# Three pairs of down units per late expert and MLP group as seven half-size products

## The chip, the cores and the metric

The kernel runs on one core of a Trainium2 chip. The metric is the device time of one execution in microseconds (us). The engines are TensorE (PE, with its weight loads PEld), VectorE (DVE), ScalarE (ACT), GpSimd (POOL) and SyncE (SP), which issues the transfers. The median of the kernel before is 3008.59 us over 3 runs, 3008.18 to 3008.73.

## What is computed

The reference is two transformer-like blocks over 512 tokens of 1024 features, in float32. The first has attention, retention and a feed-forward over 16384 experts (`peer_ffn`); the second has an RWKV-7 branch, a convolution, attention over a memory and an ordinary MLP. The two parts that matter here both have the form "multiply up, activate, scale, multiply down, add to x":

```python
# experts (each token gates 8 heads x 16 of the 16384 experts; all others have gate 0)
act = jax.nn.gelu(jnp.einsum('thkd,td->thk', u, xb), approximate=False)
out = jnp.einsum('thk,thkd->td', gate * act, v)
# MLP of the second block
x = x + jnp.square(jax.nn.relu(hm @ w_up)) @ w_down
```

## The kernel before

All of x lies in SBUF as 8 chunks of 128 features by 512 tokens (`x`, C = 8, P = 128, T = 512). The experts are computed densely: all 16384 in 16 groups of 1024, with the gates of the tokens in a table that is zero where an expert isn't chosen. The MLP has 4 groups of 1024 hidden features.

A weight unit is 128 x 1024 floats: 8 chunks of 128x128. `Weights` (L52 on) holds a ring of RING = 4 raw units. A unit is split into two parts of a shorter float format, because a product is then three fast matmuls: ScalarE copies it into the high part (`hi_step`, L142), VectorE subtracts to get the low part (`lo_step`, L150), and TensorE multiplies high x high, high x low and low x high for each of the 8 chunks (`multiply`, L184; `multiply_chunk`, L170), 24 matmuls of 512 tokens. The input side has high and low parts too (`act_hi`, `act_lo`, `inner_hi`, `inner_lo`). High and low parts are made AHEAD = 2 units before their use. SyncE loads the next unit into a raw slot once the low part of the unit that was in it is made (`load`, L111).

`feed_forward` (L1591 on) runs the last 8 of the 16 expert groups and all 4 MLP groups. Each group has 16 units: first 8 up units into PSUM banks 0 to 3, then 8 down units into banks 4 to 7, one per output chunk of x. For each up unit VectorE scales the product by `rstd` (L1705), ScalarE applies the activation (L1675), VectorE multiplies by the gate (experts) or by itself (MLP) (L1717), ScalarE copies the high part (L1677), and VectorE subtracts the low part (L1719), into chunk k of `inner`. For each down unit VectorE adds the PSUM bank to its chunk of x (L1726). The two activation tiles `raw_act` and `raw_gated` each have two buffers. All orders are written out by hand: an engine has one loop over the groups, each wait names a count of a semaphore, and the value is computed in the loop. The last group of each call is written out separately, with the first steps of what follows it (`following`, the RWKV input) or ends it (`final`). On SyncE each expert group also loads the gates of the next group, 2 MB (L1616), after the load of its 16th unit. GpSimd has nothing in these groups.

What stands ahead: in the early expert groups (`stored_groups`) GpSimd multiplies stored up products by `rstd` (L1819). In the RWKV part, GpSimd multiplies convolution inputs (L2354). In the gate stage GpSimd multiplies one-hot tiles (L1473), while VectorE makes others from a PSUM tile (L1556, L1563). In the memory attention units are multiplied with 256 tokens (L184 with `branch_hi`).

## Time and profile before

| | |
|---|---|
| median of 3 runs | 3008.59 us |
| span of the profiled execution | 3009.3 us |
| TensorE busy | 2968.3 us (99%), 15858 matmuls |
| VectorE busy | 1718.1 us (57%) |
| ScalarE busy | 1063.5 us (35%) |
| GpSimd busy | 440.2 us (15%) |
| high part of a unit, ScalarE L142 | 459 times, 1053 ns each |
| low part of a unit, VectorE L150 | 399 times, 1258 ns each |
| down products of late groups, L170 with inner | 3 x 1024 matmuls, 395 ns each |

The span is from the first to the last instruction of one execution taken by the profiler; it lies 0.7 us above the median of the runs. A matmul's record is longer than its share of time, as matmuls are pipelined: their distance from start to start counts. The 8 late expert groups begin at about 1231 us of the span and take 89.6 us each; the MLP groups lie between 2641 and 2996 us.

### The profile page before, as it was taken

To read this page: it belongs to the slowest core of one execution; us is meant where nothing else is said; L and a number is where in the kernel's file an instruction comes from. 1 tells how busy PE (TensorE), PEld (TensorE's weight loads), DVE (VectorE), ACT (ScalarE), POOL (GpSimd) and SP (SyncE) were. 2 spreads that over 40 slices of the span, in tenths; PEclk is the share of its full clock that TensorE was granted. 3 is DMA by queue.
4 is the path that set the end of the run, shared out by engine and by line. 5 is a ranking of instruction groups with operands and counts; after the bars stand their busy time and mean duration, and the time that the engine had idled before them with its cause. 6 is when DMAs were issued, how large, how long until landed. Compare 5 with 4: busy or idle time off the path is not lost. (4 is left out here: it accounts for less than half of the span.)

```text
span 3009.3 us, 42541 instructions
## 1 busy us (share of the span) xinstructions
PE 2968.3 (99%) x15858; PEld 2378.4 (79%) x15858; DVE 1718.1 (57%) x3031; ACT 1063.5 (35%) x1537; POOL 440.2 (15%) x317
## 2 busy tenths in 40 slices
PE   9999999999999999999999999999999999999998
PEld 7656888889978888788888888786896888778886
DVE  4665389999836556444444444666455464544444
ACT  3355123244443433222233322424225252433222
POOL 0200055565542231000000000020220000000000
PEclk9999999999999999999999999999999999999999
DMA  4212234455575464333333233322002233222221
GB/s 141 91 52 72 83 113 129 144 183 223 223 266 189 159 216 174 96 126 118 125 125 120 83 125 125 93 89 65 28 3 84 91 119 112 71 90 92 86 95 70
DMA packets 107065, 353.03 MB, mean 117 GB/s; under 512 B 11682, under 2 KB 12706, under 8 KB 105411
## 3 DMA queue, kind: packets, MB, share of 16 engines
q1 hardware_dynamic: 106946, 351.42, 34.8%
q8 instruction: 79, 1.29, 0.2%
q14 instruction: 40, 0.32, 0.0%
HBM read 298.95 MB, written 52.43 MB: 117 GB/s over the span
## 5 line engine op out<-in xcount | busy, mean ns | idle before, releaser
L142 ACT ACTIVATE weights_hi<-weights_raw 128x1024 fp32r<-128x1024 f32 x459 | 479.9, 1053 | 759.1 <-PE psum L170 386.9
L184 PE MATMUL psum<-act_hi,weights_hi 128*128 128x512 f32 x1592 | 632.0, 397 | 4.2 <-PEq L1317 1.7
L184 PE MATMUL psum<-act_lo,weights_hi 128*128 128x512 f32 x1592 | 628.9, 395 | 0.0
L184 PE MATMUL psum<-act_hi,weights_lo 128*128 128x512 f32 x1592 | 628.8, 395 | 0.0
L150 DVE TENSOR_TENSOR weights_lo<-weights_raw,weights_hi 128x1024 fp32r<-128x1024 f32 x399 | 500.2, 1258 | 105.7 <-ACT weights_hi L142 105.3
L170 PE MATMUL psum<-inner_hi,weights_lo 128*128 128x512 f32 x1024 | 404.5, 395 | 0.0
L170 PE MATMUL psum<-inner_hi,weights_hi 128*128 128x512 f32 x1024 | 404.5, 395 | 0.0
L170 PE MATMUL psum<-inner_lo,weights_hi 128*128 128x512 f32 x1024 | 404.5, 395 | 0.0
L184 PEld LDWEIGHTS psum<-act_hi,weights_hi 128*128 128x128 f32 x1592 | 298.4, 187 | 80.5 <-issue 7.7
L184 PEld LDWEIGHTS psum<-act_lo,weights_hi 128*128 128x128 f32 x1592 | 298.5, 187 | 73.2 <-issue 1.2
L184 PEld LDWEIGHTS psum<-act_hi,weights_lo 128*128 128x128 f32 x1592 | 298.4, 187 | 73.0
L1726 DVE TENSOR_TENSOR x<-x,psum 128x512 f32<-128x512 f32 x96 | 66.1, 688 | 304.8 <-PE psum L170 304.8
L170 PEld LDWEIGHTS psum<-inner_hi,weights_lo 128*128 128x128 f32 x1024 | 191.9, 187 | 47.1
L170 PEld LDWEIGHTS psum<-inner_lo,weights_hi 128*128 128x128 f32 x1024 | 191.9, 187 | 47.0
L170 PEld LDWEIGHTS psum<-inner_hi,weights_hi 128*128 128x128 f32 x1024 | 191.9, 187 | 46.9
L150 POOL TENSOR_TENSOR weights_lo<-weights_raw,weights_hi 128x1024 fp32r<-128x1024 f32 x44 | 116.2, 2648 | 271.4 <-ACT weights_hi L142 271.4
L1402 PEld LDWEIGHTS psum<-hot 128*128 128x128 f32 x1024 | 133.8, 191 | 12.2
L2055 POOL TENSOR_TENSOR gates_of_group<-rwkv_projections 128x512 f32<-128x512 f32 x15 | 22.2, 1483 | 783.2 <-DVE rwkv_projections L2017 783.2
L1402 PE MATMUL psum<-hot 128*128 128x128 f32 x1024 | 134.7, 274 | 0.0
L1819 POOL TENSOR_TENSOR up_group<-up_group,rstd 128x512 f32<-128x512 f32 x64 | 95.2, 1524 | 221.7 <-DMA up_group<-ups_dram 219.9
L1556 DVE TENSOR_TENSOR hot<-psum,picks_t 128x512 f32<-128x512 f32 x192 | 125.4, 688 | 3.4 <-PEq L1391 2.2
L1876 DVE TENSOR_TENSOR x<-x,psum 128x512 f32<-128x512 f32 x64 | 44.1, 689 | 144.3 <-PE psum L170 144.3
(425 smaller groups left out, 4378.0 us busy)
## 6 DMA issues: line engine op xcount, KB each, us to landing
weights_raw<-in_u_experts SPq DMA_DIRECT2D x256, 512.0 KB, 3.6
gates_dram<-gates_stage SPq DMA_DIRECT2D x8, 4096.0 KB, 12.2
gates_of_group<-gates_dram SPq DMA_DIRECT2D x16, 2048.0 KB, 11.8
weights_raw<-in_u_mlp SPq DMA_DIRECT2D x64, 512.0 KB, 3.4
ups_dram<-up_products SPq DMA_DIRECT2D x64, 256.0 KB, 2.2
up_group<-ups_dram SPq DMA_DIRECT2D x8, 2048.0 KB, 8.9
weights_raw<-in_u_in SPq DMA_DIRECT2D x24, 512.0 KB, 4.2
weights_raw<-in_u_merge SPq DMA_DIRECT2D x24, 512.0 KB, 3.6
```

The lines of the kernel that those rows point to most:

```text
L142: self.nc.scalar.activation(self.hi[slot][:, :, :], self.raw[:, slot, :].rearrange("p (c n) -> p c n", c=C), ACT.Copy).then_inc(self.hi_re ...
L150: eng.tensor_tensor(self.lo[slot][:, :, :], self.raw[:, slot, :].rearrange("p (c n) -> p c n", c=C), self.hi[slot][:, :, :].bitcast(F32), ...
L170: mm = self.nc.tensor.matmul(out, w[slot][:, c, :], a[:, c, :], start=c == 0 and n == 0, stop=c == C - 1 and n == 2)
L184: mm = self.nc.tensor.matmul(out, w[slot][:, c, :], a[:, j, 0:tokens], start=first and n == 1, stop=last and n == 3 * len(chunks))
L1402: mm = nc.tensor.matmul(psum[:, k, t * P:(t + 1) * P], hot1[c % HOTS][:, t, :], hot2[c % HOTS][:, t, :], start=True, stop=True)
L1556: return nc.vector.tensor_tensor(hot[:, :, :], places_of_keys.unsqueeze(1).to_broadcast([P, QUAD, P]), picks_t[:, r, bass.ds(i * LOOP_TOKE ...
L1726: nc.vector.tensor_tensor(x[:, d, :], x[:, d, :], psum[:, 4 + d % RING, :], ALU.add).then_inc(out_free.sem, 1)
L1819: nc.gpsimd.tensor_tensor(group[:, c, :], group[:, c, :], rstd[:], ALU.mult).then_inc(ups_scaled.sem, 1)
L1876: nc.vector.tensor_tensor(x[:, d, :], x[:, d, :], psum[:, 4 + d % RING, :], ALU.add).then_inc(out_free.sem, 1)
L2055: nc.gpsimd.tensor_tensor(self.diff[:, n % 2, :], rw[:, n, 0:T], rw[:, n, 1:T + 1], ALU.subtract).then_inc(shift_diff.sem, 1)
```

## The change

In `feed_forward` every group but the last of each call keeps its 8 up units and its first PLAIN = 2 down units. The other six down units form PAIRS = 3 pairs, A (units 10, 11), B (12, 13) and C (14, 15). A pair is a matrix of 2 x 2 weight blocks (two output chunks by the even and the odd halves of the inner chunks) times a matrix of 2 x 2 blocks of the inner activations (even and odd chunks by two halves of 256 tokens). Instead of eight block products it takes seven, by Winograd's form of Strassen's scheme. Each product is 4 x 3 = 12 matmuls of 256 columns. The names are P1 to P7; A11, A12 are the blocks of the upper unit, A21, A22 of the lower; S1 = A21 + A22, S2 = S1 - A11, S3 = A11 - A21, S4 = A12 - S2 are the weight sums, T1 to T4 the token sums.

What each engine does in such a group:

- GpSimd: 4 weight sums per pair, 128x512 each, from the raw units (`weight_sums`).
- VectorE: per pair of inner chunks one subtraction of 512 elements and two of 256 (`token_sums`) in the activation buffers, then one low part of 1024 elements (`tokens_lo`); per pair of units one low part of 1024 and five of 512; per pair five adds of 256 and one of 512 to x.
- ScalarE: one high part of 1024 elements per pair of inner chunks (`tokens_hi`); per pair of units one of 1024 and five of 512.
- TensorE: 8 up units, 2 plain down units, 3 x 84 matmuls of 256 columns, in a written order that interleaves the pairs.

The high and low parts of S1 and A22 lie in the ring's slot of the lower unit; S2, S3 and S4 have tiles of their own, which are laid where the RWKV and the convolution tiles lie later or lay before. The gate is applied in place, and `raw_act` and `raw_gated` together are now four buffers. In the first call the small RWKV loads wait until the last group has begun, and so do GpSimd's first steps of what follows.

```diff
-                        for d in range(C):
-                            pe.wait_ge(out_free.sem, i * C + (base + d + 1))
-                            bank = psum[:, 4 + d % RING, :]
-                            for c in range(C):
-                                if d == 0:
-                                    pe.wait_ge(ffn_lo.sem, i * C + (h0 + c + 1))
-                                mm = w.multiply_chunk(pe, i, C + d, per, bank, (h_hi, h_lo), c)
-                            mm.then_inc(w.unit_done.sem, 1)
+                    def product(out, weight, part, start=False, stop=False):
+                        for q in range(Q):
+                            for n, (a, b) in enumerate(((0, 0), (0, 1), (1, 0))):
+                                mm = nc.tensor.matmul(out, weight(q)[a], part(q)[b], start=start and q == 0 and n == 0,
+                                                       stop=stop and q == Q - 1 and n == 2, skip_group_check=True)
+                        return mm
...
+                    def p5(i, p):
+                        after(pe, fast_lo, LOWS, i, p, "S1")
+                        if p == A_:
+                            pe.wait_ge(t_lo_ready.sem, i * Q + (t_lo_ready.base + Q))
+                        product(beside(p, 1), unit_part(slots_of(p)[1], 0), token_sum(T1), start=True).then_inc(fast_product.sem, 1)
...
+                    def p6(i, p):
+                        after(pe, fast_lo, LOWS, i, p, "S2")
+                        after(pe, fast_read, READS, i, p, 1)
+                        product(chain(p), weight_sum(2), token_sum(T2)).then_inc(fast_product.sem, 1)
...
+                    def group(i, lead=None):
+                        ups(i, lead)
+                        for d in range(PLAIN):
+                            plain(i, d, RING - 2)
+                        p1(i, A_)
+                        p5(i, A_)
+                        p6(i, A_)
+                        p2(i, A_)
+                        p3(i, A_)
+                        p1(i, B_)
+                        p7(i, A_)
+                        p5(i, B_)
+                        p6(i, B_)
+                        p4(i, A_)
+                        p2(i, B_)
+                        p3(i, B_)
+                        p1(i, C_)
+                        p7(i, B_)
+                        p5(i, C_)
+                        p6(i, C_)
+                        p4(i, B_)
+                        p2(i, C_)
+                        p7(i, C_)
+                        p3(i, C_)
+                        p4(i, C_)
...
+                    def token_sums(i, q):
+                        pair = raw_pair(q)
+                        upper, lower = (pair[:, n, :].rearrange("p (h t) -> p h t", h=2) for n in range(2))
+                        dve.wait_ge(ffn_lo.sem, i * C + (h0 + 2 * q + 2))
+                        nc.vector.tensor_tensor(upper, pair[:, :, H:T], upper, ALU.subtract).then_inc(t_first.sem, 1)
+                        dve.wait_ge(t_first.sem, i * Q + (t_first.base + q + 1))
+                        nc.vector.tensor_tensor(lower[:, 1, :], lower[:, 1, :], upper[:, 0, :], ALU.subtract).then_inc(t_second.sem, 1)
+                        dve.wait_ge(t_second.sem, i * Q + (t_second.base + q + 1))
+                        nc.vector.tensor_tensor(lower[:, 0, :], lower[:, 0, :], lower[:, 1, :], ALU.subtract).then_inc(t_summed.sem, 1)
...
+                    def fast_body(i):
+                        for k in range(C):
+                            scale(i, k)
+                            if k and k % 2 == 0:
+                                token_sums(i, k // 2 - 1)
+                            elif 1 < k < C - 1:
+                                tokens_lo(i, k // 2 - 1)
+                            gate(i, k)
+                            if k < C - 1:
+                                w.lo_step(dve, i, k + w.AHEAD, per)
+                            inner_lo_step(i, k)
+                        w.lo_step(dve, i, C - 1 + w.AHEAD, per)
+                        tokens_lo(i, Q - 2)
+                        a1_lo(i, A_)
+                        token_sums(i, Q - 1)
+                        add_plain(i, 0)
+                        s1_lo(i, A_)
+                        a22_lo(i, A_)
+                        tokens_lo(i, Q - 1)
+                        s2_lo(i, A_)
+                        add_plain(i, 1)
+                        add_p1(i, A_)
+                        s4_lo(i, A_)
+                        add_p5(i, A_)
+                        s3_lo(i, A_)
+                        a1_lo(i, B_)
+                        s1_lo(i, B_)
+                        a22_lo(i, B_)
+                        add_u2(i, A_)
+                        s2_lo(i, B_)
+                        add_upper(i, A_)
+                        s4_lo(i, B_)
+                        add_p1(i, B_)
...
+                    def weight_sums(i, p):
+                        (k0, k1), (slot0, slot1) = units_of(p), slots_of(p)
...
+                        loaded(pool, i, k0)
+                        loaded(pool, i, k1)
+                        if p:
+                            after(pool, fast_lo, LOWS, i, p - 1, "S1")
+                        nc.gpsimd.tensor_tensor(s1, a21, a22, ALU.add).then_inc(s_summed.sem, 1)
+                        if p:
+                            after(pool, fast_lo, LOWS, i, p - 1, "S2")
+                        after(pool, s_summed, SUMS, i, p, 1)
+                        nc.gpsimd.tensor_tensor(s2, s1, a11, ALU.subtract).then_inc(s_summed.sem, 1)
+                        if p:
+                            unit_ready(pool, w.lo_ready, i, units_of(p - 1)[1])
+                        nc.gpsimd.tensor_tensor(s3, a11, a21, ALU.subtract).then_inc(s_summed.sem, 1)
+                        after(pool, s_summed, SUMS, i, p, 2)
+                        nc.gpsimd.tensor_tensor(s4, a12, s2, ALU.subtract).then_inc(s_summed.sem, 1)
```

## Rows read from the trace of the kernel before

**Rows 1.** Page, busy time: us, share of the span, instructions.
```profile
PE 2968.3 (99%) x15858; PEld 2378.4 (79%) x15858; DVE 1718.1 (57%) x3031; ACT 1063.5 (35%) x1537; POOL 440.2 (15%) x317
```

**Rows 2.** Busy time by stretch: stretch, length, each engine's busy us, clock, DMA share, GB/s.
```profile
1455.20:1500.00 44.80, 44.80 (x194) 35.99 (x193) 17.02 (x19) 10.61 (x11) 0.00 (x0) 1.00 0.45 152
1410.40:1455.20 44.80, 44.80 (x194) 35.99 (x193) 22.54 (x29) 15.51 (x21) 0.00 (x0) 1.00 0.27 82
```

**Rows 3.** Chain in order of time, two halves of MLP groups: start, us, what.
```profile
2725.93 44.80 PE psum L184 x192
2770.73 44.80 PE psum L170 x192
```

**Rows 4.** Timeline, first and last of 96 matmuls: start, us, engine, line, operation.
```profile
2464.56 0.28 PE L184 MATMUL psum<-branch_hi,weights_hi 128*128 128x256 f32 x1
...
2475.64 0.28 PE L184 MATMUL psum<-branch_hi,weights_lo 128*128 128x256 f32 x1
```

**Rows 5.** Timeline of VectorE, then ScalarE, after an eighth up unit (over at 1455.20).
```profile
1455.39 0.69 DVE L1705 TENSOR_TENSOR inner_activated<-psum,rstd 128x512 f32<-128x512 f32 x1 [1.78 <-PE psum L184]
1456.78 0.69 DVE L1717 TENSOR_TENSOR inner_gated<-inner_activated,gates_of_group 128x512 f32<-128x512 f32 x1 [0.70 <-ACT inner_activated L1675]
1458.17 0.69 DVE L1719 TENSOR_TENSOR inner_lo<-inner_gated,inner_hi 128x512 fp32r<-128x512 f32 x1 [0.70 <-ACT inner_hi L1677]
1458.78 2.36 DVE L150 TENSOR_TENSOR weights_lo<-weights_raw,weights_hi 128x1024 fp32r<-128x1024 f32 x2
...
1456.11 0.63 ACT L1675 ACTIVATE inner_activated<-inner_activated 128x512 f32<-128x512 f32 x1 [2.28 <-DVE inner_activated L1705]
1457.50 0.63 ACT L1677 ACTIVATE inner_hi<-inner_gated 128x512 fp32r<-128x512 f32 x1 [0.76 <-DVE inner_gated L1717]
1458.04 1.99 ACT L142 ACTIVATE weights_hi<-weights_raw 128x1024 fp32r<-128x1024 f32 x2
```

**Rows 6.** Timeline, a VectorE operation of 256 elements.
```profile
2479.65 0.42 DVE L3311 TENSOR_TENSOR conv_out<-psum,memory_rstd 128x256 f32<-128x256 f32 x1 [1.31 <-PE psum L184]
```

**Rows 7.** One line's instructions, GpSimd L1819: ns minimum/median/maximum.
```profile
L1819 POOL TENSOR_TENSOR up_group<-up_group,rstd x64: 1279/1296/2307, 848.4 to 1162.1; 128x512 f32<-128x512 f32 x64
```

**Rows 8.** Timeline of VectorE, then GpSimd, in an early expert group.
```profile
972.61 2.13 DVE L150 TENSOR_TENSOR weights_lo<-weights_raw,weights_hi 128x1024 fp32r<-128x1024 f32 x1
...
972.36 1.29 POOL L1819 TENSOR_TENSOR up_group<-up_group,rstd 128x512 f32<-128x512 f32 x1 [33.00 <-DMA up_group<-ups_dram]
...
973.61 2.27 POOL L1819 TENSOR_TENSOR up_group<-up_group,rstd 128x512 f32<-128x512 f32 x1
```

**Rows 9.** Timeline of VectorE and GpSimd in the RWKV part (first and last of four).
```profile
2089.43 0.69 DVE L2285 TENSOR_TENSOR rwkv_b<-rwkv_b,decay_inverse 128x512 f32<-128x512 f32 x1
2089.60 3.47 POOL L2354 TENSOR_TENSOR conv_projections<-conv_projections 128x512 f32<-128x512 f32 x1 [24.76 <-DVE conv_projections L2297]
...
2091.24 0.69 DVE L2288 SCALAR_TENSOR_TENSOR rwkv_kk<-rwkv_kk,decay_before 128x512 f32<-128x512 f32 x1
2092.01 2.14 DVE L150 TENSOR_TENSOR weights_lo<-weights_raw,weights_hi 128x1024 fp32r<-128x1024 f32 x1
```

**Rows 10.** GpSimd L1473 (ns minimum/median/maximum), and busy time in its stretch.
```profile
L1473 POOL TENSOR_TENSOR hot<-hot,picks_t x64: 1038/1040/1047, 619.9 to 819.2; 128x512 f32<-128x512 f32 x64
...
700.00:750.00 50.00, 50.00 (x348) 45.77 (x347) 49.63 (x110) 24.42 (x40) 26.02 (x28) 1.00 0.56 218
```

**Rows 11.** Timeline, TensorE waiting for VectorE in the memory attention.
```profile
2589.75 0.69 DVE L3330 TENSOR_TENSOR inner_lo<-psum,inner_hi 128x512 fp32r<-128x512 f32 x1 [4.35 <-ACT inner_hi L3245]
...
2590.50 0.50 PE L184 MATMUL psum<-inner_hi,weights_hi 128*128 128x512 f32 x1 [0.98 <-DVE inner_lo L3330]
```

**Rows 12.** DMA issues (KB each, median us to landing), and a gate load's issue.
```profile
weights_raw<-in_u_experts SPq DMA_DIRECT2D x256, 512.0 KB, 3.6
...
gates_of_group<-gates_dram SPq DMA_DIRECT2D x16, 2048.0 KB, 11.8
...
1463.67 0.39 SPq L1616 DMA_DIRECT2D gates_of_group<-gates_dram  x1
```

More of the change, by code:

```diff
@@ L1621, in _ @@
                             w.load(sp, (groups - 1) * per + k + RING, v % RING, dram, index)
+                        if following and k == RING:
+                            sp.wait_ge(w.unit_done.sem, fast_groups * per + w.done(-1))
+                            following.load(sp)
                     if following:
@@ new lines, in beside, with p1 @@
+                    def beside(p, half):
+                        return psum[:, (5, 7)[p % 2 == 0], half * H:(half + 1) * H]
+                    def p1(i, p):
+                        pe.wait_ge(out_free.sem, i * C + (base + RING + 2 * p))
+                        after(pe, fast_lo, LOWS, i, p, "A1")
+                        product(chain(p), unit_part(slots_of(p)[0], 0), block_of(0, 0), start=True).then_inc(fast_product.sem, 1)
+                    def p5(i, p):
[3 more added lines that the diff above has]
+                        product(beside(p, 1), unit_part(slots_of(p)[1], 0), token_sum(T1), start=True).then_inc(fast_product.sem, 1)
@@ L1652, in _ @@
                         group(0, preceding)
-                    with pe.Fori(1 if preceding else 0, groups) as i:
+                    with pe.Fori(1 if preceding else 0, fast_groups) as i:
                         group(i)
+                    ups(fast_groups)
+                    for d in range(C):
+                        plain(fast_groups, d, RING - 2 if d < 2 else RING if d < RING else d + 1)
                     if following:
@@ L1697, in _, with scale, gate @@
                 def _(dve):
-                    def body(i, last):
+                    def scale(i, k):
+                        dve.wait_ge(w.unit_done.sem, i * per + w.done(k))
+                        nc.vector.tensor_tensor(raw(k), psum[:, k % RING, :], rstd[:], ALU.mult).then_inc(read.sem, 1)
+                    def gate(i, k):
+                        dve.wait_ge(activated.sem, i * C + (a0 + k + 1))
+                        if gates and k == 0:
+                            dve.wait_ge(gates_loaded.sem, i * 16 + (gates_loaded.base + 16))
+                        one = raw(k)
+                        other = gate_tile[:, :, k * GT:(k + 1) * GT] if gates else one
+                        if gates:
+                            one = one.rearrange("p (b t) -> p b t", t=GT)
+                        nc.vector.tensor_tensor(one, one, other, ALU.mult).then_inc(gated.sem, 1)
@@ new lines, in add_plain, with part_of, chain, beside @@
+                    def add_plain(i, d):
+                        dve.wait_ge(w.unit_done.sem, i * per + w.done(C + d))
+                        nc.vector.tensor_tensor(x[:, d, :], x[:, d, :], psum[:, 4 + d % RING, :], ALU.add).then_inc(out_free.sem, 1)
+                    def part_of(p, row, half):
+                        return x[:, units_of(p)[row] - C, half * H:(half + 1) * H]
+                    def chain(p):
+                        return psum[:, (4, 6)[p % 2 == 0], 0:H]
+                    def beside(p):
+                        return psum[:, (5, 7)[p % 2 == 0], :]
@@ L1699, in body, with last_body @@
+                    def last_body(i):
                         for k in range(per):
                             def lo_ahead():
-                                if not (last and w.u0 + (groups - 1) * per + k + w.AHEAD >= w.total):
+                                if not w.u0 + i * per + k + w.AHEAD >= w.total:
                                     w.lo_step(dve, i, k + w.AHEAD, per)
                             if k < C:
-                                dve.wait_ge(w.unit_done.sem, i * per + w.done(k))
@@ L1723, in body @@
                             else:
-                                d = k - C
-                                dve.wait_ge(w.unit_done.sem, i * per + w.done(k))
-                                nc.vector.tensor_tensor(x[:, d, :], x[:, d, :], psum[:, 4 + d % RING, :], ALU.add).then_inc(out_free.sem, 1)
-                                if last and d:
-                                    chunk(d - 1)
+                                add_plain(i, k - C)
+                                if k > C:
+                                    chunk(k - C - 1)
                     def sums(c):
```

296 lines of the change are left out of this document (251 added, 45 removed).

## The prediction

> **What bounds the kernel now.** I read the page's busy table first: the reader is to see that TensorE is busy for 99% of the span [rows 1]. Then the busy time by stretch, for the two halves of one late expert group: TensorE is busy 44.80 of 44.80 us in each, at a granted clock of 1.00 (the 2.4 GHz level), while VectorE is busy 17 to 22.5 us, ScalarE 10.6 to 15.5 and GpSimd 0 [rows 2]. The chain in order of time shows the same without gaps in the MLP groups: 192 matmuls in 44.80 us, up half after down half [rows 3], so one 128x512 matmul costs 44.80/192 = 0.2333 us and one weight unit (24 matmuls) 5.60 us. In these groups only TensorE's stream sets the time; the others have slack, and they can become late.
>
> **What is removed.** The change runs in 7 expert groups and 3 MLP groups (the last of each stays as it was), three pairs of down units in each: 30 pairs. A pair was 48 matmuls of 512 columns, 48 x 0.2333 = 11.20 us. It becomes 7 products of 12 matmuls with 256 columns. Everything hangs on their price, since each still needs its own 128x128 weight load. The trace of before has such matmuls in the memory keys: 96 starts from 2464.56 to 2475.64, all with weight loads, 11.08/95 = 0.1166 us each [rows 4], half of 0.2333. A pair then costs 84 x 0.1166 = 9.80 us and saves 1.40 us: 4.20 a group, 42.0 in all. A bound above: if the 0.187 us record of a load were the spacing, a pair would be 15.7 us; rows 4 exclude it for a stream without register-computed waits, and one wait in 12 matmuls I cost at nothing, as the present down half, which waits for its inner chunks in the same manner, runs without a gap [rows 3].
>
> The Trainium skill (TensorE: Matmul & The Clock Gate, "Back-to-back issue gap") gives N/2.4 + 2.5 ns, 109 and 216 ns for 256 and 512 columns; by it 30 pairs would save 30 x (48 x 0.2158 - 84 x 0.1092) = 35.6 us. This trace has 117 and 233 ns, and they decide.
>
> **What is added.** Durations, as record / distance to the next start on the engine: VectorE 512 elements 0.69/0.60, 1024 elements 1.22/1.14; ScalarE 512 0.63/0.53, 1024 1.04/0.95 [rows 5]; VectorE 256 0.42/0.33, the record from [rows 6], the distance an estimate by the same 0.09 overlap. GpSimd with two real 128x512 inputs 1.29, 1.25 when queued [rows 7]. A consumer starts 0.03 us after a VectorE or ScalarE record ends, and 0.20 after a unit's last matmul slot [rows 5].
> VectorE per group: 4 token sums (one 512 and two 256, each waiting for the one before: 1.6 us), 4 low parts of 1024, three more low parts of 512 net per pair, and six adds for two. Its work after the last up unit becomes about 30 us in a stretch that should last 40.6. ScalarE gains 4 x 1.04 and about 2 us a pair, some 10 us, and stays under half busy. GpSimd gets 12 sums, 12 x 1.25 = 15 us, where it had none.
>
> Without interference I followed one group, with 0 at the end of the eighth up unit. VectorE: scale, gate, low part of the 8th chunk to 3.65; the low parts of unit 9 to 4.8 (due 5.6), of the third token sum to 6.0, of A's upper unit to 7.1; the last token sum to 8.7; an add, S1 and A22 low parts, and then the last token low part at 12.8. P5 of pair A wants it at 11.2 + 1.4 = 12.6: 0.25 late; P6 wants the add of P1 and is 0.2 late; all later waits have 0.6 to 4 us to spare. That is 0.45 us a group and the least I can find: -37.5 us.
>
> **The interference.** GpSimd and VectorE share something. A VectorE subtraction of two SBUF tensors that started at 972.61, under a GpSimd multiply of 972.36, took 2.13 instead of 1.22 us; the next GpSimd multiply took 2.27 instead of 1.29 [rows 7, 8]. One waits until the other is through. Yet VectorE operations that read PSUM and one SBUF tensor cost nothing: with VectorE busy 49.63 of 50 us the GpSimd multiply stays at 1038 to 1047 ns [rows 10]. And when VectorE runs back to back it keeps its turn: four 512 operations 0.60 apart from 2089.43 on held a GpSimd multiply to 3.47 us, and the first VectorE operation behind a gap (2092.01) then took 2.14 [rows 9].
> The Trainium skill (SBUF — State Buffer, "Who interferes with whom") has this as one exclusive lock between a VectorE instruction with two SBUF inputs and a GpSimd one that reads SBUF. The trace agrees in all three groups.
>
> All new operations but the adds and scales are of the kind that waits. So the group again, with that rule. The load of unit 11 lands 3.6 us [rows 12] behind the low part of unit 7, at -3.6, and pair A's four weight sums start there, in the seventh chunk's work. VectorE's run holds the first to -1.0; the second goes beside a scale; the third gets in ahead of the gate of the 8th chunk and delays it from 1.6 to 2.7, the fourth its low part to 4.4, which ends at 5.1. The first plain unit wants that at 4.9 and the second wants its low part at 5.94 and gets it at 6.2: stalls of 0.34 and, the second, 0.43 (with 0.06 us and an estimated 0.1 for a restart in each [rows 11]). The last token low part is ready at 14.1 instead of 12.8, P5 of A wants it at 13.4 by then: 0.86. Pair B's sums are held by VectorE's runs; its third waits for the S3 low part of A (18.1), is held to 20.2, the fourth ends at 23.2, the S4 low part it feeds at 25.0, with the add of P1 queued behind it, which P6 of B wants at 24.1: 1.44. Pair C's have 1 to 4 us to spare. Stalls 0.34 + 0.43 + 0.86 + 1.44 = 3.1 of 4.2: a gain of 1.1 us a group, 11 us in all.
>
> **Moved at no cost.** The small loads behind the experts now wait on SyncE at the fifth load of the last expert group until the group before is done; that has happened by then, as that load itself waits for a low part made in this group, and their first reader is a group away. The gate load (2 MB) on the same queue goes out at about 18.5 instead of 8.5 us after the up units, as the load of unit 15 ahead of it waits for pair A's S3; with 11.8 us to land [rows 12] it is there at 30, and the unit behind it, which ScalarE wants at 34.7, by 32. If that cover went, up to 2 us a group would be due in the next group's first unit. The banks and the doubled activation buffers take waits away where TensorE had none.
>
> **Sum.** The profiled span is 3009.3 us; 30 x 1.40 = 42.0 less 10 x 3.1 = 31 gives 2998.3, and the span is 0.7 above the median of the runs, so 2998, rounded. Bounds of the stalls: 0.45 a group (no interference) and, below, 5.5. I take 3.1 because the trace's one case of a GpSimd request against a running VectorE queue [rows 9] is what this schedule has most.
>
> **Rivals.**
> 1. The sums fall into gaps: GpSimd's requests come while VectorE waits for ScalarE or adds from PSUM, and delay nothing late. Stalls 0.45: 3009.3 - 37.5, 2972. For it: 20 of VectorE's operations after the up units are adds from PSUM; against: the pair A burst falls where VectorE is densest. 0.28.
> 2. Slower: GpSimd gets in at every change from one VectorE instruction to the next, not only at gaps. Then pair A's sums go before the gate, the unit-8 low part and the low part of the seventh chunk, which ends at 2.6 instead of -0.9; unit 8 is 0.9 late, unit 9 0.45, P5 of A 2.0, P7 of A 1.3, P6 of B 0.8: 5.5 a group with the restarts, and 10 x 1.3 = 13 slower, 3022. It decides where the low part of unit 8 ends after 0. Against: rows 9. 0.24.
> 3. The half-width products cost more than half here, through waits whose values are computed in the loop or through the loads. At the 0.187 us of a load 30 x 4.5 = 135 slower, 3144; 0.125 instead of 0.1166 would take back 21. Against: rows 4. 0.04, 0.03 of it for the dear end.
> The forecast has 0.44, with 2988 to 3009 as its own range.
>
> **Range and chances.** From rival 1 to rival 2, 2970 to 3022, which leaves out some 0.15. A difference below 0.2% (6 us) can't be told from no change in this kernel: faster 0.56 (rival 1, and 0.28 of the forecast's 0.44), within 0.14, slower 0.30 (rivals 2 and 3 and 0.02 of the forecast).
>
> **What would show it.** The 256-column matmuls of the experts at 0.117 us start to start, 252 a group, or not. The group's length from first up matmul to first up matmul: 89.6 before; 88.5 by the forecast, 85.9 by rival 1, 90.9 by rival 2. TensorE's idle time in the down half by releaser: the token low part, the add of P1, and unit 9's low part about 1 us each. GpSimd's weight sums above 1.29 us and VectorE's gates and low parts above 0.69 and 1.22 in the same stretches; if neither is lengthened there, the interference was the wrong step. If stalls end at ScalarE or at a load of weights instead, my chain is wrong in its engine.

## The result and the profile after

The changed kernel takes 3025.48 us (median of 4 runs, 3023.71 to 3029.73) against 3008.66 for the kernel before on the same chip: ratio 1.0056, 95% interval 1.0042 to 1.007. It is slower; the forecast was 2998 us with a range of 2970 to 3022. The profiled execution took 3029.73 us, its span is 3027.9 us, 18.6 more than before. Of these, 16.5 lie in the ten changed groups (12.5 in the seven expert groups, 4.0 in the three MLP groups) and agree with the 16.8 us of the medians; 2.0 lie in the first 300 us, ahead of the change, and are not its doing (the granted clock from 200 to 300 us was 0.98 in this execution and 1.00 in the one before).

The page's busy table after answers to [rows 1]:

```profile
PE 2945.7 (97%) x16938; PEld 2407.4 (80%) x16938; DVE 2005.1 (66%) x3431; ACT 1155.0 (38%) x1697; POOL 645.4 (21%) x437
```

TensorE's busy time fell by 22.6 us and the span grew: it now waits. Busy time by stretch, about one whole expert group in each line (columns as in [rows 2]):

```profile
1329.60:1421.20 91.60, 87.00 (x494) 74.62 (x493) 68.80 (x88) 35.29 (x48) 20.24 (x12) 1.00 0.36 114
1421.20:1511.80 90.60, 87.11 (x494) 74.70 (x493) 67.59 (x88) 35.31 (x48) 20.75 (x12) 1.00 0.37 116
```

Before, such a group took 89.6 us and TensorE had no idle time in it. The granted clock is 1.00, the 2.4 GHz level, as before, so the clock has no part in this. GpSimd's 12 sums take 20.2 us where 12 x 1.25 = 15.0 were expected. TensorE's waits by releaser over the whole kernel, those of the changed down halves (us in total, times, longest):

```profile
PE psum L1717 <- DVE token_sums_lo L1934: 16.9, 10, 1.7
PE psum L182 <- DVE weights_lo L162: 12.4, 18, 1.8
PE psum L1717 <- DVE x L1991: 9.7, 10, 1.0
...
PE psum L1717 <- DVE x L1983: 0.9, 1, 0.9
PE psum L182 <- DVE branch_lo L1920: 0.7, 1, 0.7
```

In the main they are the last token low part (P5 of pair A), the low parts of units 8 and 9, and the add of P6 that P7 of pair A waits for. All five lines are waits for VectorE, 40.6 us together. GpSimd's sums and two of VectorE's lines (ns minimum/median/maximum):

```profile
L2113 POOL TENSOR_TENSOR weight_sums<-weights_raw x30: 1284/1575/1829, 1274.6 to 2902.2; 128x512 f32<-128x512 f32 x30
...
L2120 POOL TENSOR_TENSOR weight_sums<-weights_raw x30: 1286/2205/2284, 1277.7 to 2906.3; 128x512 f32<-128x512 f32 x30
...
L1916 DVE TENSOR_TENSOR inner_gated<-inner_gated,gates_of_group x32: 681/686/1789, 1252.4 to 1919.3; 128x512 f32<-128x512 f32 x32
...
L162 DVE TENSOR_TENSOR weights_lo<-weights_raw,weights_hi x339: 1207/1218/2332, 8.3 to 2997.8; 128x1024 fp32r<-128x1024 f32 x170
```

The largest GpSimd record is 1.00 us above its smallest, less than one VectorE operation of 1024 elements takes (1.14). The single records say it directly: 96 of the 120 sums are longer than 1.34 us, and in each of the 96 exactly one VectorE operation with inputs in SBUF, already in progress when the sum began, ended during the wait. In 58 of them VectorE's next such operation was queued right behind; in all 58 GpSimd went first, and that next operation ended 0.54 us or more after the sum. How that looks in time, in the seventh chunk of the group of the first window:

```profile
1365.33 1.29 POOL L2113 TENSOR_TENSOR weight_sums<-weights_raw 128x512 f32<-128x512 f32 x1 [54.36 <-DMA weights_raw<-in_u_experts]
1365.35 1.55 DVE L1930 TENSOR_TENSOR inner_activated<-inner_activated 128x256 f32<-128x256 f32 x1
1366.70 1.36 POOL L2117 TENSOR_TENSOR weight_sums<-weight_sums,weights_raw 128x512 f32<-128x512 f32 x1
1366.83 1.78 DVE L1916 TENSOR_TENSOR inner_gated<-inner_gated,gates_of_group 128x512 f32<-128x512 f32 x1
1368.03 1.73 POOL L2120 TENSOR_TENSOR weight_sums<-weights_raw 128x512 f32<-128x512 f32 x1
1368.54 2.30 DVE L162 TENSOR_TENSOR weights_lo<-weights_raw,weights_hi 128x1024 fp32r<-128x1024 f32 x1
...
1369.71 2.26 POOL L2122 TENSOR_TENSOR weight_sums<-weights_raw,weight_sums 128x512 f32<-128x512 f32 x1
1370.76 1.76 DVE L1920 TENSOR_TENSOR inner_lo<-inner_gated,inner_hi 128x512 fp32r<-128x512 f32 x1
```

Read the ends: GpSimd's first ends at 1366.62, VectorE's 256 elements (0.42 alone) at 1366.90, GpSimd's second at 1368.06, the gate (0.69 alone) at 1368.61, and so on in turns. The records of these four VectorE operations add up to 7.39 us; alone they would be 0.42 + 0.69 + 1.22 + 0.69 = 3.02.

### The profile page after: what moved, and what is told of

It reads as the page before. It is cut to its first block and busy times, and to the rows that moved or that the text cites. A ratio compares the mean times of both kernels' runs of the same rounds, so it can differ in the third digit from the quotient of the medians.

```text
span 3027.9 us, 46324 instructions
## 1 busy us (share of the span) xinstructions
PE 2945.7 (97%) x16938; PEld 2407.4 (80%) x16938; DVE 2005.1 (66%) x3431; ACT 1155.0 (38%) x1697; POOL 645.4 (21%) x437
## 3 DMA queue, kind: packets, MB, share of 16 engines
q8 instruction: 88, 1.44, 0.2%
## 5 line engine op out<-in xcount | busy, mean ns | idle before, releaser
L162 DVE TENSOR_TENSOR weights_lo<-weights_raw,weights_hi 128x1024 fp32r<-128x1024 f32 x339 | 438.4, 1296 | 113.4 <-ACT weights_hi L154 113.0
L182 PE MATMUL psum<-inner_hi,weights_hi 128*128 128x512 f32 x688 | 274.0, 398 | 10.0 <-DVE weights_lo L162 10.0
L2113 POOL TENSOR_TENSOR weight_sums<-weights_raw 128x512 f32<-128x512 f32 x30 | 45.4, 1514 | 1093.6 <-DMA weights_raw<-in_u_mlp 545.3
L182 PE MATMUL psum<-inner_hi,weights_lo 128*128 128x512 f32 x688 | 271.8, 395 | 0.0
L182 PE MATMUL psum<-inner_lo,weights_hi 128*128 128x512 f32 x688 | 271.7, 395 | 0.0
L182 PEld LDWEIGHTS psum<-inner_hi,weights_hi 128*128 128x128 f32 x688 | 128.9, 187 | 49.3 <-DVE weights_lo L162 16.1
L182 PEld LDWEIGHTS psum<-inner_hi,weights_lo 128*128 128x128 f32 x688 | 129.0, 187 | 31.5
L182 PEld LDWEIGHTS psum<-inner_lo,weights_hi 128*128 128x128 f32 x688 | 129.0, 188 | 30.5
L2257 DVE TENSOR_TENSOR x<-x,psum 128x512 f32<-128x512 f32 x64 | 44.0, 688 | 142.8 <-PE psum L182 142.6
L1461 ACT ACTIVATE gates_stage<-psum 128x512 f32<-128x512 f32 x128 | 76.4, 597 | 102.0 <-PE psum L1414 102.0
## 6 DMA issues: line engine op xcount, KB each, us to landing
gates_of_group<-gates_dram SPq DMA_DIRECT2D x16, 2048.0 KB, 12.1
```

Source lines behind the costliest of these rows:

```text
L162: eng.tensor_tensor(self.lo[slot][:, :, :], self.raw[:, slot, :].rearrange("p (c n) -> p c n", c=C), self.hi[slot][:, :, :].bitcast(F32), ...
L182: mm = self.nc.tensor.matmul(out, w[slot][:, c, :], a[:, c, :], start=c == 0 and n == 0, stop=c == C - 1 and n == 2)
L1461: nc.scalar.activation(stage[:, half, :, n % GSTEPS * QUAD:(n % GSTEPS + 1) * QUAD], psum[:, c % 2, :].rearrange("p (t j) -> p j t", t=QUA ...
L2113: nc.gpsimd.tensor_tensor(s1, a21, a22, ALU.add).then_inc(s_summed.sem, 1)
L2257: nc.vector.tensor_tensor(x[:, d, :], x[:, d, :], psum[:, 4 + d % RING, :], ALU.add).then_inc(out_free.sem, 1)
```

## Experiments

Theory L: the lock of [rows 8], with GpSimd next after each VectorE instruction in progress (rival 2 of the prediction; its first texts add the condition that these instructions carry waits and updates, which the benches below took away). Rivals: V, VectorE is late by its own added work; M, the half products cost more than half; and the forecast's own turn rule, by which VectorE back to back is not interrupted.

**The weight sums cut to 4 columns.** Each sum covers 4 blocks of 128 columns; here it takes 4 columns of each, 16 elements instead of 512. The rest is set to zero once.

```
+ a11, a12, a21, a22, s1, s2, s3, s4 = (t[:, :, 0:4] for t in (a11, a12, a21, a22, s1, s2, s3, s4))
  nc.gpsimd.tensor_tensor(s1, a21, a22, ALU.add).then_inc(s_summed.sem, 1)
```

> The kernel after, with GpSimd's twelve sums per group on 4 of their 128 columns each (the rest of the sums stays zero, so the late products are wrong numbers); order, waits and VectorE's work are unchanged. Theory L (the two engines wait for each other on operations with two SBUF inputs, and GpSimd gets in between any two operations of VectorE that carry waits and updates): the waits of TensorE on the low part of the tokens (1.7 us a group), on the add of P6 of pair A (1.0) and on the low parts of units 8 and 9 (1.2) all but vanish, groups go from 91.4 to about 86.0 to 86.5 us, and the time is 2968 to 2982 us; no VectorE operation of 512 elements with SBUF inputs takes over 1.0 us. Rival V (VectorE is late by its own added work of 24 token operations a group, whatever GpSimd does): the waits stay, 3010 to 3025 us. Rival M (half products cost more than half): 3015 us or more with no waits left.

Measured: 2976.25 us (2974.43 to 2978.84), ratio to before 0.989, interval 0.9875 to 0.9906. The changed groups' waits on weights_lo, on the tokens' low part and on the adds are gone from TensorE's list. A window of 86 us shows TensorE without a gap, and VectorE's 88 operations in 59.33 us instead of 68.80:

```profile
1324.00:1410.00 86.00, 86.00 (x493) 74.78 (x492) 59.33 (x88) 35.14 (x49) 6.79 (x12) 1.00 0.39 122
```

So GpSimd's sums cost 3025.48 - 2976.25 = 49 us, and 9.5 us of VectorE's time a group were waiting. V and M fall as causes of the loss: with the same VectorE operations and the same half products the waits are gone. The run also comes near the time of rival 1 of the prediction (2972): a group takes 86.1 us from first up matmul to first up matmul, where rival 1 had 85.9.

**The sums on VectorE, in the order at hand.**

```
+ nc.vector.tensor_tensor(out, one, other, op).then_inc(s_summed.sem, 1)
...
  a22_lo(i, A_)
+ weight_sum(i, A_, 4)
  tokens_lo(i, Q - 1)
  s2_lo(i, A_)
+ weight_sum(i, B_, 1)
  add_plain(i, 1)
  add_p1(i, A_)
```

> The kernel after, with the twelve weight sums on VectorE, at places of its order where it has slack (pair A's among the last inner chunks and after a22, those of B and C in the tail between the adds); GpSimd idle. Theory L: VectorE gains 12 x 0.69 = 8.3 us of work a group and loses some 10 us of waiting for GpSimd; waits of TensorE fall from 3.9 us a group to under 1.0, 2975 to 2990 us. Rival V: VectorE is the limit already, its work in the stretch around P5 of A grows by 2 to 3 us and the wait there grows with it: 3030 to 3060 us.

Measured: 3006.42 us (3004.82 to 3010.04), ratio 0.999, interval 0.9981 to 0.9999. It lies between L's range and V's: 19 us better than the kernel after, 30 worse than the small sums. TensorE's waits say where:

```profile
PE psum L1717 <- DVE x L1983: 15.7, 20, 2.2
PE psum L1717 <- DVE token_sums_lo L1934: 5.7, 10, 0.7
```

The add of P1 frees the bank that P6 writes. P1 of A had ended at 1380.8 in one group; the add came at 1383.05, behind the sum and the plain add that I had put or left ahead of it:

```profile
1381.85 0.68 DVE L2025 TENSOR_TENSOR weight_sums<-weights_raw 128x512 f32<-128x512 f32 x1
1382.45 0.68 DVE L1970 TENSOR_TENSOR x<-x,psum 128x512 f32<-128x512 f32 x1
1383.05 0.41 DVE L1983 TENSOR_TENSOR x<-x,psum 128x256 f32<-128x256 f32 x1
...
1383.51 0.39 PE L1717 MATMUL psum<-token_sums_hi,weight_sums_hi 128*128 128x256 f32 x1 [0.44 <-DVE x L1983]
```

**The low part of the unit ahead before the token sums.**

```
  if k and k % 2 == 0:
+     w.lo_step(dve, i, k + w.AHEAD, per)
      token_sums(i, k // 2 - 1)
...
- if k < C - 1:
+ if k < C - 1 and (k == 0 or k % 2):
      w.lo_step(dve, i, k + w.AHEAD, per)
```

> The kernel after, with one order changed on VectorE: in chunks 2, 4 and 6 the low part of the unit ahead goes before the token sums and not behind the gate. Theory L: the low parts of units 8 and 9 start about 2 us sooner, so 12.4 us of TensorE's waits in 18 places go down to 3 or less; the low part of the last tokens stays late, since the alternation with GpSimd around it is untouched: 3012 to 3020 us. Rival V (order and amount of VectorE's work set the lateness): about the same at unit 9, but the token sums that are put back delay the inner low parts, 3020 to 3035 us.

Measured: 3028.71 us (3025.04 to 3030.26), ratio 1.0065, interval 1.005 to 1.008. That is outside L's range and inside V's. The waits on units 8 and 9 went from 12.4 to 1.8 us, as L said, but they came back in the inner low parts that now stood behind, as V said (11.8 us, and 3.1 more in the MLP groups). So order and amount of VectorE's work do set where the lateness falls; the run with small sums had shown that without GpSimd's sums there is none.

```profile
PE psum L1717 <- DVE token_sums_lo L1934: 12.4, 10, 1.7
PE psum L182 <- DVE inner_lo L1920: 11.8, 7, 1.7
PE psum L1717 <- DVE x L1991: 9.7, 10, 1.0
...
PE psum L182 <- DVE weights_lo L162: 1.8, 10, 0.3
```

A wait that comes from several held-up operations in a row was not removed by changing which of them is last.

**A first bench of the two engines.** Eight VectorE and six GpSimd additions of 128x512 at a time; VectorE's loop, with the wait and the update there or not:

```
for k in range(8):
    dve.wait_ge(loaded, 64)
    nc.vector.tensor_tensor(vout[:, k, :], a[:, 0, :], b[:, 0, :], ALU.add).then_inc(vstep, 1)
```

> A bench that computes nothing of the reference: nine sections in which VectorE issues 8 additions of 128 x 512 elements while GpSimd issues 6 of them, all with two SBUF inputs unless told. VectorE's have neither wait nor update between them (section 0), an update each (1), a wait each that is long met (2), both (3), both and one input in PSUM (4), both against GpSimd's without either (5), both with GpSimd idle (6); 7 is GpSimd alone; 8 repeats 0. Theory L-wait: in 0 and 1 VectorE keeps its turn: 8 in about 5.5 us, GpSimd's held until they are done; in 2 and 3 they take turns, each VectorE operation 0.7 to 2.0 us and each GpSimd one 1.3 to 2.0. Theory L-update: turns already in 1. Rival B (the four that ran undisturbed in the kernel before were chance): turns in 0 as well. In 4 all agree on no effect: VectorE about 0.7 us each, GpSimd 1.29. In 6 0.69 each, in 7 1.29.

Timeline of VectorE, eight operations to a line:

```profile
10.54 13.47 DVE L57 TENSOR_TENSOR s_plain_vs_wi<-in_a,in_b 128x512 f32<-128x512 f32 x8
24.12 13.22 DVE L57 TENSOR_TENSOR s_i_vs_wi<-in_a,in_b 128x512 f32<-128x512 f32 x8
37.44 13.24 DVE L57 TENSOR_TENSOR s_w_vs_wi<-in_a,in_b 128x512 f32<-128x512 f32 x8
...
62.17 4.87 DVE L57 TENSOR_TENSOR s_wip_vs_wi<-psum,in_b 128x512 f32<-128x512 f32 x8
```

Eight took 13.2 to 13.5 us (1.65 to 1.68 for each pair of VectorE and GpSimd) with neither waits nor updates, with updates and with waits, and 4.87 with one input in PSUM, as [rows 10] had it. (With both, 11.29: there GpSimd's six stood beside VectorE's eight.) So rival B of that text: turns in every form. The bench had a flaw: GpSimd ran a section ahead, so its sections without a partner (6 and 7) ran against each other and show nothing of their own; the next bench mends that.

**The sums on VectorE, in a better order.** P1's adds, which free the bank that P6 writes, no longer stand behind plain adds and several sums, and A's sums stand among the last chunks. The edit against the run that took 3006 us, in part:

```
  tokens_lo(i, 3)
+ add_plain(i, 0)
  s2_lo(i, A_)
  weight_sum(i, B_, 1)
- add_plain(i, 1)
  add_p1(i, A_)
- weight_sum(i, B_, 2)
  s4_lo(i, A_)
  add_p5(i, A_)
...
```

> The weight sums on VectorE as in the run before (3006.42 us), in another order of VectorE's instructions from the seventh chunk on: A's sums among the chunks, the low part of the last tokens ahead of the first add of the plain units, and each add that frees the chain's bank (P1's) at once behind the product it reads instead of behind sums and adds that nobody waits for yet. If the 3006 us were left over from order alone (waits of TensorE of 15.7 us on the add of P1 in 20 places and 5.7 us on the low part of the tokens in 10, each with a slow restart, beside 18.2 us of the weight loads' waits), these go below 5 us in sum and the time is 2972 to 2980 us, as with the small sums (2976.25). If VectorE's amount of work is the limit (80 us of 87 a group is not, but 28 us in a stretch of 29 behind the chunks is near it), the waits only move to other places: 2990 to 3005 us.

Measured: 2972.13 us (2971.22 to 2972.82), ratio 0.9877, interval 0.9861 to 0.9894. It beats both kernels. Two groups, and the chain's row for the half products of one group:

```profile
1236.70:1322.45 85.75, 85.75 (x494) 74.72 (x493) 65.45 (x100) 35.20 (x48) 0.00 (x0) 1.00 0.40 123
1322.45:1408.20 85.75, 85.75 (x494) 74.73 (x493) 65.45 (x100) 35.20 (x48) 0.00 (x0) 1.00 0.40 122
```

```profile
2750.29 29.76 PE psum L1716 x252
```

TensorE is busy all of 85.75 us again, and VectorE is busy 65.45 us with 100 operations, less than the 68.80 that 88 took beside GpSimd. 252 half-width matmuls take 29.76 us, 0.1181 each.

**Only pair A's sums small.**

```
+ if p == A_:
+     a11, a12, a21, a22, s1, s2, s3, s4 = (t[:, :, 0:4] for t in (a11, a12, a21, a22, s1, s2, s3, s4))
```

> The kernel after, with GpSimd's four sums of pair A alone on 4 of their 128 columns (those of B and C whole; the products of pair A are wrong numbers). The lock of A's sums meets VectorE in chunks 5 to 7, where units 8 and 9 and the last tokens' low part are made; that of B's and C's meets it in the tail. If lateness comes from the chunks (theory of A's sums): the waits on units 8 and 9 (12.4 us in all) and nearly all of the 16.9 us on the tokens' low part go, the 9.7 us on P6's add of A stay in part, 2984 to 2996 us. If it comes from the tail: those waits stay, 3010 to 3020 us.

Measured: 3000.13 us (2996.76 to 3001.47), ratio 0.9967, interval 0.9954 to 0.9979: by difference 25 of the 49 us go with A's four sums and 24 with the eight of B and C. The time lies between the two ranges of that text. Its theory of A's sums had the waits on units 8 and 9 right (gone), and that on P6's add as well (9.8 us), but not that on the tokens' low part:

```profile
PE psum L1718 <- DVE token_sums_lo L1935: 10.7, 10, 1.2
PE psum L1718 <- DVE x L1992: 9.8, 10, 1.0
```

```profile
1375.96 1.68 POOL L2116 TENSOR_TENSOR weight_sums<-weights_raw 128x512 f32<-128x512 f32 x1 [11.72 <-DVE weights_lo L1947]
...
1376.40 2.33 DVE L1935 TENSOR_TENSOR token_sums_lo<-inner_gated,token_sums_hi 128x1024 fp32r<-128x1024 f32 x1
```

It is B's first sum that holds the tokens' low part up: 2.33 us here, and in the changed kernel too, where that operation took 2.31 us from 1383.68 on beside B's sum of 1383.24. A's sums only added the lateness with which it began.

**The better order, with the sums back on GpSimd.** VectorE's list of the 2972 us kernel without its weight_sum lines; GpSimd's block as in the change.

> The kernel after with VectorE's order of the run that took 2972 us, its twelve sums a group taken out of VectorE's list again and left on GpSimd as in the kernel after. If the order was the fault and the sharing only came on top, this order has slack enough to bear it: 2985 to 3000 us. If the lock is the fault (each of GpSimd's 12 sums holds VectorE up for 1.0 to 1.3 us a group, 12 to 15 us, where doing them on VectorE costs 12 x 0.60 = 7.2 us), the order gives back only the waits on P6's add (9.7 us) and a part of the tokens' low part: 3000 to 3020 us.

Measured: 2997.12 us (2995.86 to 2998.72), ratio 0.9962, interval 0.9948 to 0.9976. Order alone gives back 28 us and makes the change, with its sums still on GpSimd, a gain of 0.4%; the sums on GpSimd instead of VectorE then still cost 2997.12 - 2972.13 = 25 us. The time lies in the range for the order, near its upper end and 3 us below the range for the lock. The two don't share the loss as two separate parts: in the old order, with GpSimd's sums small, the kernel took 2976.25 us, so the old order costs next to nothing by itself. It turns the hold-ups into waits of TensorE. Taking the hold-ups away gives back 49 us, a better order 28. The waits left:

```profile
PE psum L181 <- DVE weights_lo L161: 7.4, 8, 1.7
PE psum L181 <- DVE inner_lo L1919: 7.2, 7, 1.1
PE psum L181 <- DVE branch_lo L1919: 4.7, 3, 2.0
```

**A second bench, with one GpSimd addition at a time.** The first line releases GpSimd, the second is VectorE's run of five:

```
nc.vector.tensor_tensor(vout[:, 7, :], psum[:, :], b[:, 0, :], ALU.add).then_inc(go, 1)
nc.vector.tensor_tensor(vout[:, k, :], vout[:, k, :], b[:, 0, :], ALU.add)
```

> A bench that computes nothing of the reference: GpSimd's addition of 128 x 512 elements comes about 0.1 us into the first of five of VectorE's, all with two SBUF inputs: VectorE's without wait and update between them (section 0), with an update each (1), a wait each (2), both (3), neither and in place (4), both and in place (5), three of 1024 elements with both (6), 0 again (7); 8 is VectorE alone, six with both; 9 seven in place without either against five of GpSimd's in a row; 10 GpSimd alone. The stretch of before in which GpSimd waited 2.2 us for four of VectorE's was of form 4. Theory W (a wait or an update opens the turn): GpSimd's takes 4.0 to 4.4 us in 0, 4 and 7, and 1.7 to 1.9 in those forms that open it. Theory A (after the instruction in progress it is always GpSimd's turn, as in the first bench where both had work queued from the start): 1.7 to 1.9 in 0 to 5 and 7, 2.3 in 6, and VectorE's second takes 1.7 to 1.9 in each. Theory I (in place keeps the turn): long in 4, 5 and 9 alone. In 8 VectorE's take 0.69 with 0.60 from one to the next.

Sections 3 and 4 (both wait and update; neither, in place), and VectorE alone:

```profile
24.85 4.15 DVE L63 TENSOR_TENSOR s_wi_by<-in_a,in_b 128x512 f32<-128x512 f32 x5
25.01 1.64 POOL L82 TENSOR_TENSOR pool_out<-in_c,in_d 128x512 f32<-128x512 f32 x1 [3.16 <-DVE s_wi_by L55]
...
31.45 4.16 DVE L63 TENSOR_TENSOR s_o_by<-s_o_by,in_b 128x512 f32<-128x512 f32 x5
31.61 1.64 POOL L82 TENSOR_TENSOR pool_out<-in_c,in_d 128x512 f32<-128x512 f32 x1 [4.96 <-DVE s_o_by L55]
...
52.84 3.69 DVE L63 TENSOR_TENSOR s_wi_by<-in_a,in_b 128x512 f32<-128x512 f32 x6
```

GpSimd's took 1.56 us in the first section, 1.64 in the six others with one of GpSimd's beside 512 elements, and 2.17 beside 1024: its own 1.26 and what was left of the operation in progress. Theory A of that text, in all forms, a little below its 1.7 to 1.9 us.

**A third bench: the forms of the odd stretch.** As the second, with these for the run, and GpSimd in place:

```
nc.vector.tensor_tensor(res, res, two, ALU.mult)
nc.vector.scalar_tensor_tensor(res, res, -1.0, two, ALU.mult, ALU.mult)
```

> A bench that computes nothing of the reference: as the second bench (GpSimd's one operation comes 0.16 us into the first of five of VectorE's, which have neither wait nor update between them), with the forms of the stretch of before in which GpSimd waited 2.2 us for four operations: products for sums, in place on VectorE, in place on GpSimd, a second operand from another place each, a scalar_tensor_tensor as the last, an operation of 1024 elements behind them; singly and together, and sections 7 and 9 with sums. If one of these forms keeps VectorE's turn, GpSimd's takes 3.4 to 4.4 us from that section on and 1.64 in the others; if none does, 1.64 everywhere, and the stretch of before stays unexplained.

Measured: GpSimd's took 1.57 or 1.58 us in all ten sections. No form keeps the turn.

**In the kernel before: the four operations small; the four with waits and updates.**

```
- nc.vector.tensor_tensor(bb[:, j, :], bb[:, j, :], back[:, j % 2, :], ALU.mult)
+ nc.vector.tensor_tensor(bb[:, j, 0:4], bb[:, j, 0:4], back[:, j % 2, 0:4], ALU.mult)
```

and in the second run

```
- nc.vector.tensor_tensor(R(K_ + j), R(K_ + j), back[:, j % 2, :], ALU.mult)
+ dve.wait_ge(scalar_read.sem, count(scalar_reads, "sums", 2 * j + 1))
+ nc.vector.tensor_tensor(R(K_ + j), R(K_ + j), back[:, j % 2, :], ALU.mult).then_inc(applied.sem, 1)
```

> The kernel before, with the four VectorE operations that stood beside the 3.47 us of GpSimd's multiplication cut to 4 of their 512 columns each (the rest of the decays isn't applied, so the RWKV outputs are wrong numbers). If VectorE's run of four held GpSimd up (the reading of the prediction), the multiplication takes 1.29 us, or up to 1.8 with part of another operation before it. If GpSimd started late by itself there, behind something of its own after 24.8 us of idling, it takes some 3.5 us again. The whole stays at 3007 to 3010 us.

> The kernel before, with a semaphore update behind each of those four VectorE operations and a wait that is long met ahead of each. By the benches the form of VectorE's operations doesn't matter: GpSimd's multiplication then shows in this place what it did before, 3.47 us, and the cause lies elsewhere. If the missing waits and updates gave VectorE its turn here after all, GpSimd gets in after the first: 1.6 to 1.9 us, and the operation of VectorE beside it 1.7 to 1.8 instead of 0.69.

Measured: 3008.39 and 3011.76 us, one run each. GpSimd's four multiplications (minimum/median/maximum) in the first, with the last of VectorE's four beside one of them, and the one at issue in the second:

```profile
L2354 POOL TENSOR_TENSOR conv_projections<-conv_projections x4: 1277/1283/1292, 2060.7 to 2123.2; 128x512 f32<-128x512 f32 x4
...
2084.40 1.28 POOL L2354 TENSOR_TENSOR conv_projections<-conv_projections 128x512 f32<-128x512 f32 x1 [22.40 <-DVE conv_projections L2297]
2084.46 1.25 DVE L2288 SCALAR_TENSOR_TENSOR rwkv_kk<-rwkv_kk,decay_before 128x4 f32<-128x4 f32 x1
```

```profile
2090.09 3.47 POOL L2358 TENSOR_TENSOR conv_projections<-conv_projections 128x512 f32<-128x512 f32 x1 [24.75 <-DVE conv_projections L2301]
```

So in that place VectorE's four did hold GpSimd up, and waits and updates have no part in it.

**A fourth bench: places and what came ahead.** The run of the third; the operand one element off is

```
res = odd[:, k, 1:T + 1]
```

> A bench that computes nothing of the reference, with twelve sections of the stretch's own sequence: an operation from PSUM that releases GpSimd, three products in place and a scalar_tensor_tensor without waits, and an operation of 1024 elements behind a wait. Plain; with the second and third one element off in rows of 513 as in the kernel (R); all four so (A); all tiles at the other end of the memory (H); GpSimd's input being what the operation from PSUM has just written (D); four more of VectorE's back to back ahead of that operation (B); and these together. If the place of an operand lets VectorE keep its turn, GpSimd's takes 3.0 to 3.6 us in every section that has that letter and 1.6 in the others; if what came ahead does, in the sections with B. If it is 1.6 in all, no form that I can copy from the stretch explains it, and the rule of the other benches (GpSimd is next after the operation in progress) stands with one exception.

Measured: GpSimd's took 1.57 us in the first section and 1.64 in the eleven others. What keeps VectorE's turn in the one place of [rows 9] stays open; I have varied the form, the operation, the place of the operands, what GpSimd reads and what VectorE did just before. In no bench did TensorE or ScalarE work beside the two.

## Why the prediction was wrong

**The saving was right, but for a small term.** 30 pairs x 1.40 = 42.0 us; measured without stalls 89.60 - 85.75 = 3.85 a group, 38.5 in all. The price of a half matmul was 0.1166, it is 0.1181: 252 x 0.0015 = 0.4 us a group. That rules rival 3 out.

**The step that failed: "when VectorE runs back to back it keeps its turn".** The whole size of the interference hung on it: 3.1 us of stalls a group. Measured: GpSimd got in after the one operation in progress in each of the 96 sums that were held, whether VectorE had its next one queued or not. The ten groups lost 16.5 us where they should have won 38.5, so the interference cost 5.5 a group, the figure of rival 2, which had GpSimd get in at every change of instruction. By places, rival 2 and the recorded waits a group: units 8 and 9 0.9 + 0.45 against 1.24; P5 of A 2.0 against 1.7; P7 of A 1.3 against 1.0; P6 of B 0.8 against 0.1. The forecast had 0.77, 0.86, none and, for P6 of B, 1.44: its largest place hardly waited at all, and it missed P7 of A. The recorded waits are 4.1 of the 5.5. Of the rest, the busy column shows most: the same 494 matmuls of a group are busy 87.00 and 87.11 us in the two windows above and 85.75 undisturbed, 1.3 us more. I take that for slow restarts behind the waits, as the prediction did in small, but no run splits it off.

**Why it failed.** One case (rows 9) was taken as the rule, and it decided between 2998 and 3022. It is real and comes back in every run that kept those four operations whole, but it is the exception: every bench section that had two SBUF inputs on both engines, and all 96 held sums of the changed kernel, have it the other way. Rows 7 and 8 could not have told: 15 of those 64 multiplications were held, each by one VectorE operation, but none of these had another of its kind queued behind it. The trace of before did hold the cases to weigh, in the token shift of the RWKV part, which neither the rows nor the prediction show. GpSimd's line there, and one case from the timeline of VectorE and of GpSimd:

```profile
L2055 POOL TENSOR_TENSOR gates_of_group<-rwkv_projections x15: 1040/1478/1953, 1963.8 to 2034.7; 128x512 f32<-128x512 f32 x15
...
1984.11 0.74 DVE L2021 SCALAR_TENSOR_TENSOR rwkv_projections<-gates_of_group,rwkv_vectors_sb,rwkv_projections 128x512 f32<-128x512 f32 x1
1984.77 1.53 DVE L2044 SCALAR_TENSOR_TENSOR x<-x,gains,gates_of_group 128x512 f32<-128x512 f32 x1
...
1984.27 1.48 POOL L2055 TENSOR_TENSOR gates_of_group<-rwkv_projections 128x512 f32<-128x512 f32 x1 [4.12 <-DVE rwkv_projections L2017]
```

VectorE runs back to back, GpSimd asks during L2021, and L2044 behind it takes 1.53 us instead of 0.74: GpSimd got in between. 12 of the 15 are such cases, against the one of rows 9.

**Interference itself** was the right step: in the stretches named, GpSimd's sums came out above 1.29 us and VectorE's gates and low parts above 0.69 and 1.22. The Trainium skill (SBUF — State Buffer, "Who interferes with whom") calls it an exclusive lock; the runs agree: in the benches a pair takes 1.65 to 1.68 us where GpSimd's alone takes 1.25 to the next and VectorE's 0.60, and VectorE's ends 0.55 us or more behind GpSimd's in every turn, as if it began only then. (1.66 is 0.19 less than 1.25 + 0.60, so a small part of the two does overlap.) Without the interference the change is 2976, near rival 1's 2972; the 4 us between them are about the 0.4 a group of the half matmuls.

**The moved gate load** cost nothing. It went out at 1390.32, 21.4 us after that group's eighth up unit (18.5 expected), took 12.1 to land, and nobody is seen to wait for it. ScalarE and the loads set no wait, as said.

**The chances.** Rival 2 had 0.24 against 0.44. With 12 cases for it and one against it in the trace of before, it was the likeliest. Its 3022 lies 3 us under the measured time because the saving it started from was 4.2 us a group and came out as 3.85.

## What to carry to other kernels

Work handed to an idle GpSimd that reads SBUF, beside a VectorE that works from SBUF, isn't free. Here 12 sums a group cost VectorE 9.5 us of waiting, where doing them itself cost it 65.45 - 59.33 = 6.1 (12 x 0.60 = 7.2 by the distances; the 59.33 still holds some waiting for the small sums). Try such work on VectorE too, and find the order: the add that frees an accumulating bank comes before sums that nobody waits for yet. When one stretch of a trace says who wins a shared resource, look up every other operation that competes for it, and among them those where the other engine had its next operation queued, before building on that stretch.

## What the runs showed of the hardware that I had not expected

- Two engines with two-SBUF-input operations queued take strict turns: 1.66 us for each pair of 128x512 fp32 operations (0.60 and 1.25 alone), whatever waits or updates VectorE's instructions carry. The waiting time is inside the record of the operation, which then shows 1.74 on VectorE and 1.59 on GpSimd (medians of the first bench).
- A GpSimd request is served after the one VectorE operation in progress, even in a back-to-back run: 1.56 to 1.64 us beside 512 elements, 2.17 beside 1024, and all 96 held sums of the changed kernel. One place in the kernel before, 3.47 us behind four operations, contradicts this in every run of the whole kernel in which those four were left at full length, and no copy of it in a bench did.
- A VectorE operation of four columns waits in full too: a scalar_tensor_tensor of 128x4 took 1.25 us beside GpSimd in the run with small decays.
